# Fifteen expert pairs by scatter and one by product, with the last pair's second weights queued behind the rows read back, in column halves

## The reference, cut to what matters

```python
for l in range(2):
    h = h + token_mixer(rms_norm(h, ln1_g[l]), w_in[l], ...)
    h = h + hier_moe(rms_norm(h, ln2_g[l]), ..., w1[l], w3[l], w2[l])
return rms_norm(h, final_g)

# hier_moe: each of 512 tokens picks one group of 8 experts, and 2 experts in it
hdn = silu(xb @ w1[e]) * (xb @ w3[e])      # 1024 -> 256
out[token] += weight * (hdn @ w2[e])       # 256 -> 1024
```

## Time and profile before

| what | value |
|---|---|
| median of 3 runs | 1525.66 us (1524.32 to 1525.85) |
| the profiled execution | 1526.16 us, its span 1524.3 us |
| busy share of the span | TensorE 91%, VectorE 28%, ScalarE 33%, GpSimd 33% |
| the chain that ended last | TensorE 73%, SyncE's queue 11%, DMA 8%, VectorE 4% |
| moved by DMA | 331.20 MB, 217 GB/s over the span |
| first layer's experts | about 505 to 764 us, DMA at 406 to 416 GB/s from 500 to 700 |
| second layer's experts | about 1252 to 1513 us, DMA at 416 GB/s from 1300 to 1400 |

### The profile page before, as it was taken

The page is one execution under the profiler, slowest core; times in us unless marked ns, Lnnn a source line. Parts: engine busy times, 40 slices in busy tenths (PEclk is TensorE's granted clock), DMA queues, the critical chain, the costliest instruction groups (busy, mean ns, idle before and its releaser), DMA issues.

```text
span 1524.3 us, 18860 instructions
## 1 busy us (share of the span) xinstructions
PE 1392.2 (91%) x7446; PEld 962.1 (63%) x7446; DVE 429.2 (28%) x1022; ACT 506.7 (33%) x843; POOL 498.7 (33%) x248
## 2 busy tenths in 40 slices
PE   5999999999999799878799999999999978988784
PEld 5889877788887333323388988777888863333232
DVE  3232644410214111110433335443112241111116
ACT  4522466622333111111253326664233322111111
POOL 4533433465641111110154433334655311111100
PEclk9999999999999799989899999999999979999997
DMA  6622222234363999999853222222434559999993
GB/s 237 243 84 84 70 69 70 74 100 159 103 230 141 388 418 416 416 416 417 320 196 135 83 84 76 70 69 70 158 105 157 235 202 390 416 417 417 415 417 125
DMA packets 133713, 331.20 MB, mean 217 GB/s; under 512 B 16085, under 2 KB 89861, under 8 KB 115192
## 3 DMA queue, kind: packets, MB, share of 16 engines
q1 hardware_dynamic: 123832, 310.08, 53.7%
q0 software_dynamic: 9792, 19.89, 3.4%
HBM read 312.16 MB, written 33.55 MB: 227 GB/s over the span
## 4 chain that ended last, share of the span: by engine, by line
PE 73%; SPq 11%; DMA 8%; DVE 4%; ACT 2%; issue 1%; POOL 0%; DVEq 0%; POOLq 0%; ACTq 0%
PE ps L505 18%; PE ps L506 17%; PE ps L507 17%; PE ps L842 10%; SPq L435 8%; DMA w<-in_w 3%; SPq L429 3%; DMA yb<-y_dram 2%; PE ps L671 2%; PE ps L651 1%; PE ps L659 1%; DMA y_dram<-yy,toks 1%; PE ps L607 1%; DMA xg<-x_dram,toks 1%; PE ps L834 1%
## 5 line engine op out<-in xcount | busy, mean ns | idle before, releaser
L505 PE MATMUL ps<-uH,ringH 128*128 128x512 f32 x720 | 281.9, 392 | 0.0
L506 PE MATMUL ps<-uL,ringH 128*128 128x512 f32 x720 | 280.4, 389 | 0.0
L507 PE MATMUL ps<-uH,ringL 128*128 128x512 f32 x720 | 280.3, 389 | 0.0
L842 PE MATMUL ps<-w,xT 128*64 128x512 f32 x1024 | 246.5, 637 | 36.3 <-DMA w<-in_w 33.8
L842 PEld LDWEIGHTS ps<-w,xT 128*64 128x64 f32 x1024 | 83.1, 147 | 196.1 <-issue 192.7
L1203 POOL TENSOR_TENSOR ringL<-raw,ringH 128x2048 fp32r<-128x2048 f32 (+1 forms) x32 | 142.7, 4464 | 122.6 <-ACT ringH L954 122.6
L505 PEld LDWEIGHTS ps<-uH,ringH 128*128 128x128 f32 x720 | 135.2, 188 | 28.9 <-issue 0.7
L507 PEld LDWEIGHTS ps<-uH,ringL 128*128 128x128 f32 x720 | 135.2, 188 | 28.7
L506 PEld LDWEIGHTS ps<-uL,ringH 128*128 128x128 f32 x720 | 135.2, 188 | 27.5
L842 PE MATMUL ps<-w,hT 128*64 128x512 f32 x512 | 121.4, 618 | 30.1 <-ACT hT L1148 30.1
L1250 POOL TENSOR_TENSOR ringL<-raw,ringH 128x2048 fp32r<-128x2048 f32 x32 | 147.0, 4595 | 5.1 <-ACT ringH L1082 5.1
(11 more groups left out here) (248 smaller groups left out, 2058.9 us busy)
## 6 DMA issues: line engine op xcount, KB each, us to landing
w<-in_w SPq DMA_DIRECT2D x192, 1024.0 KB
raw<-in_w_in SPq DMA_DIRECT2D x54, 1024.0 KB, 5.2
y_dram<-attT SPq DMA_DIRECT2D x8, 1024.0 KB, 11.7
braw<-in_w_branch SPq DMA_DIRECT2D x32, 256.0 KB, 4.5
raw<-in_w_out SPq DMA_DIRECT2D x8, 1024.0 KB, 5.3
yb<-y_dram SPq DMA_DIRECT2D x8, 1024.0 KB, 20.0
h_dram<-hs SPq DMA_DIRECT2D x2, 2048.0 KB, 11.2
hs<-h_dram SPq DMA_DIRECT2D x2, 2048.0 KB, 9.8
```

Of the source, the lines that this page charges most:

```text
L505: mm(o, h, rh, start=first, stop=False)
L506: mm(o, h, rl_, start=False, stop=False)
L507: return mm(o, l, rh, start=False, stop=last)
L842: ins = mm(o[r], lhs[:, r], rhs[x], start=first, stop=last, skip_group_check=True)
```

## The change: what it does, and the diff

- Pair 14 is scattered too (`NS` = 15). Only pair 15 is combined by products: two instead of four for each sum, 16 instead of 32 in all.
- SyncE's read back of `y_dram` waits for the scatters of pairs 0 to 14, and all four transfers are issued at once.
- w2 of pair 15 is no longer loaded ahead of the read back; it is issued behind the four `yb` transfers, as four transfers of 512 KB, the first two for columns 0 to 511, the other two for 512 to 1023. The down product of pair 15 is done half by half, as each lands.
- All sums of column half 0 go first, into four PSUM banks (`SUM_BANKS`), then those of half 1. `yH` and `yL` are made by halves.
- Unit 0 of the next layer's weights is loaded right behind w1 and w3 of pair 15; its high part moves ahead of pair 15's output on ScalarE, its low part from GpSimd to VectorE, ahead of the first `yL`. There it is one operation on 128x2048.
- On VectorE `hid` of pair 15 no longer stands behind `sum_rows(0)`. At the next norm three tiles of `ut` are made in a row before the first `uL`.
- GpSimd clears `attT` behind the split of unit 2 instead of before it.

```diff
-SLOTS, NS = 3, NP - 2
+SLOTS, NS = 3, NP - 1
+    SUM_BANKS = ((0, 1, 4, 5), (6, 7, 0, 1))
 ...
             for p in range(SLOTS, NP):
                 hold(sp, up_filled.h, up_filled.at(lay, p - SLOTS + 1))
                 w13_fill(p)
-                hold(sp, down_filled.h, down_filled.at(lay, p - SLOTS + 1))
-                w2_fill(p)
-
-            hold(sp, down_filled.h, down_filled.at(lay, NS))
+                if p < NS:
+                    hold(sp, down_filled.h, down_filled.at(lay, p - SLOTS + 1))
+                    w2_fill(p)
+
+            if lay + 1 < L:
+                hold(sp, up_filled.h, up_filled.at(lay, NP - 2))
+                sp.dma_start(raw[:, 0, :]..., w_in_cols(lay + 1, COL["gv"], 256)).then_inc(w_in_slot[0].h, 16)
+            hold(sp, down_filled.h, down_filled.at(lay, NP - 2))
             sp.dma_start(g1[:], ...).then_inc(g1_in.h, 16)
             for x in range(2):
-                hold(sp, y_stored[x].h, y_stored[x].at(lay, 16 * (NS // 2)))
+                hold(sp, y_stored[x].h, y_stored[x].at(lay, 16 * len(range(x, NS, 2))))
             for t in range(NT):
-                if t == 2:
-                    hold(sp, up_filled.h, up_filled.at(lay, NS + 1))
                 sp.dma_start(yb[t][:], y_dram[...]).then_inc(y_back[t].h, 16)
+            hold(sp, down_filled.h, down_filled.at(lay, NP - SLOTS))
+            for c in range(2):
+                for x in range(2):
+                    src = a["w2"][ds(lay, 1), ds(NS + NP * x, 1), :, c * 512:(c + 1) * 512]...
+                    sp.dma_start(w2[NS % SLOTS][x][:, :, c * 512:(c + 1) * 512], src).then_inc(w2_last_in[c].h, 16)
 ...
+            def combine_last(c):
+                hold(pe, last_low.h, last_low.at(lay, c + 1))
+                hold(pe, tokens_ready.h, tokens_ready.at(lay, 1))
+                for t in range(NT):
+                    if c and t == 2:
+                        hold(pe, half_added.h, half_added.at(lay, NT))
+                    b = SUM_BANKS[c][t]
+                    mm(bank(b), tok_of[:, tmc(t)], yH[:, c * 512:(c + 1) * 512], start=True, stop=False)
+                    mm(bank(b), tok_of[:, tmc(t)], yL[:, c * 512:(c + 1) * 512], start=False, stop=True).then_inc(sum_filled.h, 1)
 ...
+                else:
+                    for c in range(2):
+                        pe.wait_ge(w2_last_in[c].h, w2_last_in[c].at(lay, 32))
+                        down_half(s, c).then_inc(last_down.h, 1)
```

More of the change, by code:

```diff
@@ L142, in trunk @@
     yy = [sb(f"yy{x}", [P, D], f32, R_O + 4 * x * KB) for x in range(2)]
-    yH = [sb(f"yH{x}", [P, D], f32r, R_O + 4 * x * KB) for x in range(2)]
+    yH = sb("yH", [P, D], f32r, R_O + 4 * (NS % 2) * KB)
     xT = [sb(f"xT{x}", [P, D], f32, R_O + (8 + 4 * x) * KB) for x in range(2)]
@@ L855, in transpose_hidden, with down_half @@
                 return last
[L857 to L861 removed]
+            def down_half(s, c):
+                for k in range(2):
+                    w = [w2[s][x][:, k, c * 512:(c + 1) * 512] for x in range(2)]
+                    last = two_experts(bank(A[c]), hT[:, k, :], w, k == 0, k == 1)
                 return last
```

170 lines of the change are left out of this document (88 added, 82 removed).

## The result

The kernel before took 1525.64 us in this comparison (median of 5 runs, 1524.32 to 1525.85), the changed one 1533.26 (5 runs, 1531.19 to 1535.17). The ratio is 1.0051, 95% interval 1.0036 to 1.0065: slower by about 7.6 us. The forecast was 1536.5, with a range of 1530 to 1543.5.

What follows compares the result with a forecast made beforehand. The seam between experts and next layer bounds the kernel: a transfer, then VectorE, not TensorE. Terms +8.9 - 2.9 + 8.0 - 3.2 = +10.8 us on 1526.16 gave 1537.0, less 0.5 for the median: 1536.5, range 1530 to 1543.5.

Steps and rivals of the forecast that it cites:

- the forecast's case: Late w2 and a slow last down product make both layers' ends longer, 1536.5 us in all; chance 0.62.
- The sum: Both layers together: +8.9 - 2.9 in the first, +8.0 - 3.2 in the second, +10.8 us.
- the way from E: From E to the next layer's first product 15.1 us (-2.9), in the second layer to the last norm tile 15.8 (-3.2).
- E: End of pair 15's down product: forecast 759.8 instead of 750.87 (+8.9), in the second layer 1508.8 instead of 1500.8 (+8.0).
- Pair 14's down product: Unmoved by the change, ending at 732.0 and 1480.5, so pair 14's scatter is issued at 733.7 and 1482.2.
- The scatter: Pair 14's indirect store, from issue to landing: 4 us before data, 1.5 for data and completion, 5.5 in each layer.
- Rival A: The cheap scatter: pair 14's costs what a plain store does, 3.0 us; total 1531.5; chance 0.15.
- rival B: The dear scatter: pair 14's costs what loaded ones do, 9.34 and 8.37 us; total 1543.2; chance 0.10.
- The transfers behind it: Read back and w2 behind the scatter: first tile 4.5 us, then 2.53 for each further MB.
- The down product: Pair 15's 16 products on TensorE, slow after some 12 us idle: 5.9 us in the first layer, 6.37 in the second.
- Rival C: No slow clock: TensorE does pair 15's down product in 3.65 us, -2.2 and -2.7; total 1531.6; chance 0.06.
- The cover: VectorE's row sums and unit 0's low part hide beside the transfers and cost nothing, with 1.4 us to spare.

Runs made afterwards that it cites:

- x2: Changed kernel with the last pair's w2 in two whole transfers of 1 MB instead of four column halves of 512 KB; 1533.52 us, ratio 1.0053 to before.
- x4: Changed kernel with tile 0's low part behind the second norm tile, not the third; 1531.68 us, ratio 1.0040 to the kernel before.
- x6: Changed kernel with 24 unread TensorE products in each layer ahead of the wait for w2; 1537.00 us, ratio 1.0079 to the kernel before.
- x9: Changed kernel with 28 and 22 unread TensorE products (first, second layer) ahead of the wait for w2; 1535.72 us, ratio 1.0067 to before.
- x1: Changed kernel with the last pair's w2 moved back ahead of the gain and the read back; 1531.20 us, ratio 1.0034 to before.
- t4: x1 with eight PSUM banks, both `yL` between second and third row sum, unit 0's low part behind the first norm tile; 1526.66 us, ratio 1.0014 to before.
- t2: Kernel before with `hid` first, eight PSUM banks for the sums, `yL` between second and third row sum; 1516.93 us, ratio 0.9942.

## Why the prediction was right, and where its terms were off

The sign, the order of the chain and the range were right: the forecast's case held. The sum, +10.8, was 3.2 us more than the +7.6 of the medians. Step by step, against the start of pair 15's up product (the seams forecast were 42.3 and 43.0, measured 41.8 and 40.1), scatter, transfers, down product and the way from E were off by -1.5, +2.3, -0.3 and -1.0 us in the first layer and by -3.7, +2.7, -0.6 and -1.2 in the second:

- **Pair 14's down product** came 1.7 us earlier against that start in both layers, since its up product took 7.09 us, at the full clock, where the one before had 8.78. This varies from one execution to the next: x2 and x4 have 8.7 to 8.8 in the first layer, x4 in the second too. So the scatter was issued at 731.26, not 733.7.
- **The scatter**, priced 5.5 from its issue in both layers, took 5.72 and 3.33. The first looks right, but for another reason than mine. In the first layer the first `yb` issue comes 5.1 us behind the start of pair 15's up product in all five runs that have the changed queue (this one, x2, x4, x6, x9), whether the scatter was issued 0.8 us ahead of that start or 1.0 behind it, at a price of 5.72 or 4.0: so it looks as if it lands when unit 0 and the gain, which are ahead of it, are through; no run moves them to test that. I had 6.6 us there, so this step is 1.5 too late. In the second layer only the gain is ahead; there the `yb` issue follows the scatter's by 3.3 to 3.5 in all five, so here it comes at 2.4 us behind that start and not at 6.1, and the step is 3.7 too late: 2.2 of price, the rest the early issue. The 4 us before any data that I read off the loaded queues were the load: here its first data shows 1.4 us behind the issue in both layers. Rival A (3.0) was nearly right for the second layer. With w2 ahead too, the price is 6.65 and 6.97 (x1, t4), in t2's full stream 8.66: rival B's, where the queues are full.
- **The transfers behind it** were the term that was wrong in both layers: 14.6 us forecast from the first `yb` issue to the down product, 16.9 and 17.35 measured, +2.3 and +2.7. I had taken 2.53 us for every megabyte whatever its pieces; w2 in column halves moves at 250 to 320 GB/s where it starts (x2). x2 tells the pieces from the rest: by the same working w2 whole should come 17.15 us behind the first `yb` issue, and x2 has 17.7 and 18.0, which is 0.6 and 0.9 more. So the pieces account for 1.7 and 1.9 us of the 2.3 and 2.7.
- **The down product**, 5.9 and 6.37 forecast, took 5.60 and 5.74. Rival C (no slow clock) did not happen, and x9 shows that it would have been worth 0.9 and not 2.2 in the first layer, 1.6 and not 2.7 in the second. In the first the second half of w2 would have been late, which I had called free.
- **E** came 8.8 us later in the first layer by the profile's time. Counted from the start of pair 15's up product it came 9.4 later in the first (forecast 8.9) and 6.3 in the second (forecast 8.0). The first is near by errors that cancel, which is luck: -1.5 of scatter and -0.3 of the down product against +2.3 of transfers; in the second -3.7 and -0.6 stand against +2.7. I had also said that every us at the next layer's first product stays; here 3.4 of 4.9 reached the second seam.
- **The way from E** was 14.1 and 14.6 us, forecast 15.1 and 15.8. I had laid VectorE's read of the window counts in full behind the third addition; the chain has 0.5 to 0.9 us of it. x4 confirms the 1 us that the third norm tile costs ahead of the first low part.
- **The cover.** I said that each us over 1.4 on VectorE would count. VectorE ended at 754.36, the first low part was possible at 758.4: the cover was real, 4 us. But it was read as if w2 alone kept the sums waiting; x1 shows that the way over VectorE is just as long when w2 is early, so undoing the one visible cause gives back only 2.1 of 7.6 (1.7 by the seams).
- **DMA nearly idle**, expected between 737 and 741, is seen between 736 and 738 (6 GB/s). TensorE's wait ended with w2, and the first `yb` issue is at 737.14, between the 737 that I had named for rival A and the 739 of the forecast.

The Trainium skill, page "DMA: Bandwidth & Descriptors", section on the anatomy of a DMA by the gpsimd path, gives a fixed 2.0 us and the bytes at 436 GB/s; worked out from it, an estimate of 2.6 us for this scatter. The nearest measurement is 3.33 us, with the DMA at 45 to 49 GB/s when it was issued; the same scatter behind other transfers took up to 9.34. The measurement decides: the formula is a lower end, short by 0.7 even on nearly empty queues.

## What to carry to other kernels

Where two ways of nearly equal length lead to the same wait, removing the one that the chain of waits names gives back the difference only: follow the second way to its end before pricing a move, and measure a seam from a point that the change cannot touch. At a seam, first look for engines that take turns through too few buffers (two PSUM banks here; eight, with `hid` first and the low part moved, gave 8.8 us in t2) before moving work from products to transfers, because the scatter one pair later, with its read back, put some 3 us per layer on the path that t4's order did not hide. Do not put GpSimd work with SBUF operands beside VectorE work with two SBUF operands on the critical path.

## What the runs showed of the hardware that I had not expected

- The price of one indirect store of 0.26 MB, from issue to landing, was 3.33, 4.0, 5.72, 6.65, 6.97 and 8.66 us, by what other queues had in flight, and 9.34 before.
- Transfers of w2 in pieces of 2 KB moved 320 and 250 GB/s in two stretches of 2 us, in pieces of 4 KB 412 to 416 in the same place, with a DMA share of 0.90 and more in both.
- VectorE's operation with both inputs in SBUF took 4.42 and 5.40 us beside GpSimd's split in place of 1.22 and 1.28; with one input in PSUM, 0.62 each, as without it. The other way round, GpSimd's scale took 2.44 us beside VectorE's split in place of 0.56.
- Products put into a wait of TensorE right up to its end kept its granted clock at 1.00 (x9), but both kernels with them showed a pause of 2.9 to 3.1 us behind them, and their medians were 2.5 and 3.7 us above the changed kernel's (for x9, 2.5, the intervals overlap); the cause of the pause is open.
